# Modulation chunks in the router stage, and block-wise neighbourhood attention with its values reordered through DRAM

## What is computed

```python
def adaln(cond, w_mod, b_mod):
    m = jax.nn.silu(cond) @ w_mod + b_mod          # w_mod (1024, 6144) per layer
    return jnp.split(m[:, None, :], 6, axis=-1)

def neighbourhood_attention(q, k, v, k_ctx, v_ctx, rel_bias):   # 4 heads of 64
    # blocks of 16 query columns see 32 key columns kc0..kc0+31, all 8 rows
    kc0 = np.clip(j * 16 - 8, 0, 64 - 32)
    cs = np.clip(qcol - 8, 0, 64 - 16)
    col_mask = (kcol >= cs) & (kcol < cs + 16)
    s_loc = jnp.where(col_mask, q @ k_loc + bias, NEG_INF)
    s_ctx = q @ k_ctx                              # 128 cached context tokens
    pr = softmax(concatenate([s_loc, s_ctx]))
    return pr_loc @ v_loc + pr_ctx @ v_ctx
```

## Time and profile before

| | |
|---|---|
| three runs | 1847.62, 1848.31, 1857.03 us, median 1848.31 |
| the profiled execution | 1847.45 us, span 1845.6 us |
| TensorE busy | 1574.8 us (85%) |
| VectorE | 772.8 us (42%) |
| ScalarE | 471.4 us (26%) |
| GpSimd | 278.0 us (15%) |
| mean granted TensorE clock | 0.913 |
| DMA | 318.79 MB, 173 GB/s over the span |

### The profile page before, as it was taken

One profiled execution on the slowest core, in us unless ns is written; L12 is line 12 of the kernel. 1 busy time (PEld: TensorE's weight loads), 2 busy tenths in 40 slices (PEclk: granted clock), 3 DMA queues, 4 the chain that ended last, 5 costly groups with the idle time before them and its releaser, 6 DMA issues. The chain is left out here.

```text
span 1845.6 us, 23002 instructions
## 1 busy us (share of the span) xinstructions
PE 1574.8 (85%) x8725; PEld 987.4 (54%) x8725; DVE 772.8 (42%) x1586; ACT 471.4 (26%) x884; POOL 278.0 (15%) x446
## 2 busy tenths in 40 slices
PE   5899997975887976999689999996588796799993
PEld 3455554544886543444355555654488654444442
DVE  2379414454665241111254970364576524211116
ACT  1211122253322032222131111335432212222222
POOL 0200211015450012000102000001455101200002
PEclk9999999878899977999889999986798998799996
DMA  9521699913142009999581201351314200899974
GB/s 341 129 92 46 189 295 356 362 47 61 27 94 104 3 23 362 348 366 369 210 240 46 85 30 58 120 205 47 61 27 94 103 2 35 345 394 364 365 281 183
DMA packets 121264, 318.79 MB, mean 173 GB/s; under 512 B 29589, under 2 KB 39127, under 8 KB 106839
## 3 DMA queue, kind: packets, MB, share of 16 engines
q1 hardware_dynamic: 73264, 237.63, 37.4%
q0 software_dynamic: 14080, 53.48, 8.4%
q10 hardware_dynamic: 33830, 26.45, 5.2%
HBM read 250.70 MB, written 67.78 MB: 173 GB/s over the span
## 5 line engine op out<-in xcount | busy, mean ns | idle before, releaser
L741 PE MATMUL ps<-hreg,ring 128*128 128x512 f32 x768 | 396.9, 599 | 11.1 <-ACT hreg L1334 11.1
L742 PEld LDWEIGHTS ps<-hreg,ring 128*128 128x128 f32 x768 | 146.7, 191 | 185.5 <-issue 185.5
L1167 PE MATMUL ps<-ring,tok 128*128 128x512 f32 x544 | 236.4, 592 | 0.6 <-issue 0.5
L1167 PEld LDWEIGHTS ps<-ring,tok 128*128 128x128 f32 x544 | 103.2, 190 | 130.3 <-issue 130.3
L742 PE MATMUL ps<-hreg,ring 128*128 128x128 f32 x768 | 148.0, 275 | 0.0
L741 PEld LDWEIGHTS ps<-hreg,ring 128*128 128x128 f32 x768 | 117.5, 193 | 11.8 <-issue 11.8
L1182 PE MATMUL ps<-ring,work 128*128 128x512 f32 x272 | 123.4, 596 | 0.0
L2192 DVE TENSOR_TENSOR work<-work,ps 128x256 f32<-128x256 f32 x34 | 14.2, 421 | 250.5 <-ACT work L1618 250.5
L1755 DVE SCALAR_TENSOR_TENSOR mixA<-cin_reg,small,mixA 128x655 f32<-128x655 f32 x120 | 107.0, 894 | 0.0
L2196 DVE COPY zs<-ps 128x1024 f32<-128x1024 f32 x34 | 41.6, 1224 | 122.9 <-PE ps L1182 122.9
L2276 POOL TENSOR_TENSOR hreg<-dnT,cst 128x512 f32<-128x512 f32 x16 | 20.4, 1275 | 429.6 <-DVE dnT L1950 429.6
(11 more groups left out here) (353 smaller groups left out, 2630.9 us busy)
## 6 DMA issues: line engine op xcount, KB each, us to landing
ring<-in_w SPq DMA_DIRECT2D x102, 1024.0 KB, 8.7
ring<-in_w_mod SPq DMA_DIRECT2D x24, 2048.0 KB, 12.4
ring<-in_w_in SPq DMA_DIRECT2D x12, 2048.0 KB, 8.0
ys<-zs ACTq DMA_DIRECT2D x34, 512.0 KB, 7.8
tok<-xs SPq DMA_DIRECT2D x30, 512.0 KB, 11.8
xs<-zero POOLq DMA_DIRECT2D x8, 1792.0 KB, 19.7
ys<-zero POOLq DMA_DIRECT2D x8, 1664.0 KB, 20.3
ring<-diag_own SPq DMA_DIRECT2D x80, 128.0 KB, 5.2
```

Source lines behind the costliest of these rows:

```text
L741: mm(o[:, 0:TS], lhs(k), rhs(k)[:, 0:TS], start=k == 0, stop=k == nk - 1)
L742: ins = mm(o[:, TS:T], lhs(k), rhs(k)[:, TS:T], start=k == 0, stop=k == nk - 1)
L1167: ins = mm(bank(2 + q), xgT[q][:, k, :], w, start=k == 0, stop=k == KD - 1)
```

## The change

It moves and rewrites these parts:

1. **Start:** c is loaded ahead of x, and TensorE turns it first; ScalarE makes the Silu after 14 parameter DMAs, and issues three more and the bias copy (to 16 rows, not 64) behind it. VectorE makes five of layer 0's eight norm products before it copies modulation chunk 3, and clears the staging tiles after all eight, in both layers.
2. **Modulation chunks:** chunks 13, 14 and 15 leave attention for layer 0's router stage. Chunk 13 is loaded into `tok`, 14 into ring slot 1 and 15 into slot 2. ScalarE makes their copies. SP holds back expert weights until the slots are used.
3. **Attention:** a tile t is now 16 query columns by 8 rows. It sees 32 or 48 key columns (`KB0`, `KBN`: 2, 3, 3, 2 blocks of 16 columns by 8 rows), so 384 or 512 score columns with the cache. Q and K are put into block order by their eviction, the output back by its store.
4. **Values:** V leaves the projection in grid order; ScalarE stores it to DRAM (`v_rows`), waits, and loads it back as four blocks, on its own queue. TensorE's `values` waits for all of it.
5. **Bias tables:** eight loads with rows of 1,060 bytes, then 12 GpSimd additions.
6. **Zero fill:** GpSimd starts it after 6 gemms instead of 16.

The diff's core:

```diff
+ROUTER_MODS = (13, 14, 15)
 def mods_beside_attention(layer):
-    last = NMOD * (layer + 1) + (MOD_FIRST if layer + 1 < L else 0)
-    return list(range(NMOD * layer + MOD_FIRST, last))
+    return list(range(MOD_FIRST, ROUTER_MODS[0])) if layer == 0 else list(range(ROUTER_MODS[-1] + 1, 2 * NMOD))
...
# SP, router stage
                 up_load(0, 0)
                 need(mod2_ready, 2)
                 sp.dma_start(route_c, consts[:, NC:NC + NX]).then_inc(route_loaded.sem, 16)
+                if l == 0:
+                    need(gemm_done, G_OUT + 5)
+                    router_mod(13, tok_flat[:, 0:4096])
+                    router_mod(14, ring[1][:, 0:4096])
                 need(gemm_done, G_OUT + 8)
-                down_load(0, 0)
+                if l == 0:
+                    sp.wait_ge(mod_used, 14)
+                    router_mod(15, ring[2][:, 0:4096])
+                else:
+                    down_load(0, 0)
...
+                if l == 0:
+                    sp.wait_ge(mod_used, 15)
                 up_load(1, e)
+                if l == 0:
+                    sp.wait_ge(mod_used, 16)
+                    down_load(0, 0)
                 down_load(1, e)
...
# TensorE: first lines, attention, router
-            pe.wait_ge(once["first_loaded"], 64)
+            pe.wait_ge(once["cst_loaded"], 64)
+            turn(bank(4, 16), dsm[0:16, 0:P], ident[0:16, 0:16]).then_inc(once["cond_turned"], 1)
+            pe.wait_ge(once["first_loaded"], 32)
...
-                        mm(gslot(x)[:, 0:TS], qa[x], qkT[rs[x], 2 + h // 2, 0:TS], start=True, stop=True)
+                        mm(gslot(x)[:, 0:n], qa[x], qkT[rs[x], 2 + h // 2, P * KB0[t]:P * KB0[t] + n], start=True, stop=True)
...
-                    for j in range(NCH if i < 16 else 2):
+                    for j in range(KBN[i // 4] + 1 if i < 16 else 2):
                         ins = turn(ps[:, 2048 + P * j:2048 + P * (j + 1)], sc[i % 2][:, P * j:P * (j + 1)], ident)
...
                     if a < 8:
+                        need(kvc_loaded, 112)
                         need(att_ptc, 2 * a + 2)
...
                 ins.then_inc(logits.sem, 1)
+                if l == 0:
+                    mod_rows(13, 7)
+                    mod_turn(13, later_rows[1], 3200)
                 need(sel_ready, 1)
...
                 need(slots_ready, 1)
+                if l == 0:
+                    mod_rows(14, 2)
+                    mod_rows(15, 3)
+                    need(slots_ready, 2)
+                    mod_turn(14, later_rows[0], 3208)
+                    mod_turn(15, later_rows[1], 3216)
                 need(xf_loaded[0], 16)
...
# ScalarE: second norm, V, before the experts
+                        if n == 1 and l == 0 and k == 2:
+                            act.wait_ge(mod_used, 14)
+                            A_(later_rows[1], bank(7), ACT.Copy).then_inc(mod_copied, 1)
...
-                A_(vna.rearrange("p t n -> p (t n)"), ps[:, 2048:2048 + NCH * NAW], ACT.Copy).then_inc(v_copied.sem, 1)
+                A_(v_own, ps[:, 2048:2048 + 4 * NAW], ACT.Copy)
+                A_(vna[:, 4, :], ps[:, 2048 + 4 * NAW:2048 + NCH * NAW], ACT.Copy).then_inc(v_copied.sem, 1)
+                need(v_copied, 1)
+                need(kvc_loaded, 32)
+                act.dma_start(v_rows.ap()[l].rearrange("(t p) n -> p t n", p=P), v_own.rearrange("p (t n) -> p t n", t=4))\
+                    .then_inc(kvc_loaded.sem, 16)
                 need(newk_turned, 1)
                 A_(newk, ps[:, 3584:3584 + 256], ACT.Copy).then_inc(newk_copied.sem, 1)
+                need(kvc_loaded, 48)
+                for b in range(4):
+                    src = bass.AP(tensor=v_rows, offset=(l * TS + 16 * b) * NAW, ap=[[GRID * NAW, 8], [NAW, 16], [1, NAW]])
+                    act.dma_start(vna[:, b, :], src).then_inc(kvc_loaded.sem, 16)
...
+                if l == 0:
+                    for n, bnk in ((14, 2), (15, 3)):
+                        act.wait_ge(mod_used, n + 1)
+                        if n == 15:
+                            act.wait_ge(mod_turned, 14)
+                        A_(later_rows[n % 2], bank(bnk), ACT.Copy).then_inc(mod_copied, 1)
                 copy_tokens(0, 0)
                 copy_tokens(0, 1, 2048)
...
# ScalarE, eviction of Q and K
-                    evac(G_QK + t, qkT[:, t, :]).then_inc(gemm_out[t % 2].sem, 1)
+                    if t == 0:
+                        need(tz_ready, 1)
+                    out = qkT[:, t, 0:TS].rearrange("p (b r c) -> p r b c", r=8, c=16)
+                    for r_ in range(0, 8, 4):
+                        A_(out[:, r_:r_ + 4], by_block(gslot(t % 2)[:, 0:TS])[:, r_:r_ + 4], ACT.Copy)
+                    A_(qkT[:, t, TS:T], gslot(t % 2)[:, TS:T], ACT.Copy).then_inc(gemm_out[t % 2].sem, 1)
...
# VectorE: start, attention
+                early = 5 if l == 0 else 0
                 if l == 0:
                     for n in range(MOD_FIRST):
+                        if n == MOD_FIRST - 1:
+                            need(norm_r, 1)
+                            for k in range(early):
+                                norm_one(k)
                         mod_copy(n, 4 + n % 2, first_rows[n])
...
+                need(norm_r, 1)
+                for k in range(early, KD):
+                    norm_one(k)
                 for s in stage:
                     V.memset(s, 0.0)
                 V.memset(cin_reg[:, :], 0.0).then_inc(pads_zeroed.sem, 1)
...
-                        V.scalar_tensor_tensor(s[:, 0:TS], o[:, 0:TS], HD ** -0.5, Tz[:, b * GRID:b * GRID + TS], ALU.mult, ALU.add)
+                        V.scalar_tensor_tensor(s[:, 0:n], o[:, 0:n], HD ** -0.5, biases[t][:, h, :], ALU.mult, ALU.add)
...
+                if l == 0:
+                    dve.wait_ge(mod_turned, ROUTER_MODS[-1] + 1)
+                    V.tensor_copy(mod_next[:, 8:32], ps[:, 3200:3224])
# GpSimd
-                    pool.wait_ge(gemm_done.sem, gemm_done.at(0, G_Z))
+                    pool.wait_ge(gemm_done.sem, gemm_done.at(0, G_DN + 2))
```

More of the change, by code:

```diff
@@ L66, in ring_table @@
             held[s] = item
+        if layer == 0:
+            for n, s in zip(ROUTER_MODS, (2, 1, 2)):
+                count[s] += 16
+                slot[("mod", n)], value[("mod", n)] = s, count[s]
         up_base.append(list(count))
@@ L333, in build, with bias_window, by_block, att_cols @@
         tok_flat = tok[:, :, :, :].rearrange("p a c n -> p (a c n)")
[L334 to L336 removed]
+        WB = 7 * CO + 48
+        wide_bias = work[:, 0:NH * WB]
+        def bias_window(h, first, nb):
+            at0 = wide_bias[:, WB * h + first:WB * h + first + 16]
+            return bass.AP(at0.tensor, at0.offset, [at0.ap[0], [16, nb], [CO, 8], [1, 16]])
+        biases, at_ = {}, 0
+        for j in (1, 0, 3):
+            n = 8 * 16 * KBN[j]
+            biases[j] = tok_flat[:, at_:at_ + NH * n].rearrange("p (h n) -> p h n", h=NH)
+            at_ += NH * n
+        biases[2] = biases[1]
+        sc = [tok_flat[:, at_ + 512 * i:at_ + 512 * (i + 1)] for i in range(2)]
+        v_own = hreg[:, 0:4 * NAW]
+        def by_block(ap):
+            return ap.rearrange("p (r b c) -> p r b c", r=8, c=16)
+        def att_cols(i):
+            return P * KBN[i // 4]
         dflat = dnT[:, :, :].rearrange("p a b -> p (a b)")
@@ L689, in mod_rows @@
                 def mod_rows(n, bnk):
-                    w = loaded(("mod", n))[:, 0:4096].rearrange("p (k n) -> p k n", k=KD)
+                    held = loaded(("mod", n))
+                    if n == ROUTER_MODS[0]:
+                        held = tok_flat
+                    w = held[:, 0:4096].rearrange("p (k n) -> p k n", k=KD)
                     for k in range(KD):
@@ L846, in values @@
                     if a < 8:
+                        need(kvc_loaded, 112)
                         need(att_ptc, 2 * a + 2)
-                        for j in range(NCH):
+                        nb, first = KBN[a // 2], KB0[a // 2]
+                        for j in range(nb + 1):
                             for x in range(2):
                                 h = 2 * (a % 2) + x
-                                va = vna[:, j, 64 * h:64 * h + 64] if j < 4 else kvc[1][:, 64 * h:64 * h + 64]
-                                ins = mm(halves[x], va, pT_[x][:, P * j:P * (j + 1)], start=j == 0, stop=j == NCH - 1)
+                                va = vna[:, first + j, 64 * h:64 * h + 64] if j < nb else kvc[1][:, 64 * h:64 * h + 64]
+                                ins = mm(halves[x], va, pT_[x][:, P * j:P * (j + 1)], start=j == 0, stop=j == nb)
                     else:
```

139 lines of the change are left out of this document (73 added, 66 removed).

## The result

The changed kernel takes 1839.57 us (median of six runs, 1832.03 to 1843.96), the kernel before 1852.32 beside it (six runs, 1847.62 to 1857.24): a ratio of 0.9921, 95% interval 0.9892 to 0.9949. Its profiled execution took 1837.82 us (span 1836.0, mean clock 0.912), 9.63 less than that of before; forecast were 24.5. By the medians the gain is 12.8 us.

What follows compares the result with a forecast made beforehand. Expert loops and projections keep TensorE busy; the edits target four places where it waits or shares, layer 0's attention on DMA filled by zero fill. 1847.45 - 4.2 - 2.2 - 5 - 14.7 + 1.5 = 1822.9, said 1823; range 1810 to 1840.

Steps and rivals of the forecast that it cites:

- step 6: Layer 1's narrower attention: 4.4 us saved beside chunks swallowed by chunk supply, 8.7 saved after them; layer -5 us in all.
- step 7: Layer 0's attention, nine chunks instead of twelve: 80.6 us from V's end against 95.3, -14.7 us (bounds -8 and -21).
- step 5: V's trip through DRAM after the V projection: first value matmuls +6.7 us later in each layer (bounds +1 and +15).
- Step 3: Zero fill started after 6 gemms, 88 us earlier, beside input chunks loaded two ahead: costed at 0.
- Rival (b): Chunk supply bounds more, or zero fill still runs into it; half of layer 0's gain stays out: 1830, chance 0.14.
- breaking point: Sign that the forecast is wrong: a hole behind V's store of over 12 us.
- Rival (a): V's trip through DRAM is longer, 8 us a layer more than forecast: 1839, chance 0.16.
- rival (d): TensorE does not warm up in attention and its work beside chunks runs at the lower clock: 1870, chance 0.08.
- The slow part: Layer 1's attention after its last chunk: narrower score widths save 8.7 us.
- Step 8: Layer 0's router stage with chunks 13 to 15: later weight loads and scatters, +1.5 us (bounds -1 and +8).
- rival (c): Router stage: expert weights behind chunks 14 and 15 arrive late: 1830, chance 0.08.
- Steps 1, 2 and 4: Kernel start -4.2 us; layer 1's start with memsets moved behind -2.2; bias tables and reordering evictions nothing.

Runs made afterwards that it cites:

- half the bytes: Changed kernel with half of each modulation chunk's weights loaded, all matmuls kept: 1865.5 us, ratio 1.0076; put right for two extra pairs of expert blocks, 1819.8.
- the repeat: The changed kernel itself, unedited, measured once more beside the others: 1834.5 us, ratio 0.9903.
- chunk rows in the hole: Changed kernel with each modulation chunk one turn earlier, the first chunk's rows meant to run during V's trip through DRAM: 1862.2 us, ratio 1.0058.
- no trip: Changed kernel with V copied straight into the value matmuls' operand, no store or loads: 1793.8 us; put right for one fewer pair of expert blocks, 1816.7.
- ScalarE's copies first: Changed kernel with ScalarE doing two copies of turned probabilities and the third head's Exp before waiting for V's store: 1840.3 us, ratio 0.9948.

## Why the prediction was right and wrong

**The failed term** is the sum of steps 6 and 7: -19.7 predicted for the two attentions, -9.0 measured. Of the 10.7 us that are missing, 4.9 are layer 1's chunk part (step 6), 3.9 the hole behind V in both layers (step 5), 0.7 the slow part and 1.2 the rest of layer 0. Outside attention the router stage misses 2.2 us, the two starts 1.2, and 0.8 lie in stages that nobody forecast a move for.

**Step 3, the zero fill at nothing.** The mechanism was read rightly, a late chunk in layer 0 and no attention beside the fill once it is moved, and the cover held: input chunks loaded two ahead took it without a wait. But the gain was put down to the narrower attention in step 7, and the edit alone was never summed. Alone it is worth 12.5 us in layer 0's attention, more than the whole change gained there. Rival (b) took the zero fill for something that might go wrong; it was the part that went right.

**Step 5, V through DRAM, at +6.7.** Measured from the kernel before it is +8.4 and +8.9; against the changed kernel without the trip it is 9.7 and 11.7, 21 us in all, since narrower attention without the trip would have started its values sooner than before (7.9 and 6.3 for 9.2 and 9.0). Two sub-terms were short in layer 1: the store 8.2 us for 6.5, the issues 4.0 for 2.8 (the two cache stores were left out of them). The rule that store and chunk share one pool was right; the rate was not: 387 GB/s were taken, and the windows of the hole show 337 and 353. By the fit of the Trainium skill (DMA: Bandwidth & Descriptors, "Anatomy of one DMA") the hole would have been smaller than forecast; that fit holds only for the store that has no chunk beside it (above). TensorE's idle time in the hole, 11.7 and 12.3 us, stands at the bound that the prediction named as its breaking point. Rival (a), a longer trip, gives the time that was measured (1839), but by 8 us more a layer where 2 were found: right in kind, and in size by coincidence.

**Step 6, the chunk part.** Predicted 34.4 us from the first values on, measured 39.3 and 36.1; with half the bytes 34.3. What failed is "the 4.4 us are swallowed": a supply that is a little too slow can do more than swallow. It makes one wait of about 2 us, and in the changed kernel's profile 3 more go at the lower clock behind it; in the repeat they do not. So a part of the miss is chance, and what decides whether the clock falls behind such a wait no run here shows. This is rival (d) in small, where all or nothing had been asked.

**The slow part**: -8.7 predicted, -8.0 measured. **Layer 0** the same sum: 80.6 predicted, 83.5 measured. The hole is 1.7 of the 2.9; a late chunk at 331.0 (2.0 us of wait, rows at 2.46 us) can account for the other 1.2, which nothing separates.

**Step 8, the router stage**: +1.5 predicted, +3.7 measured, 3.8 given back when the chunks go back. The cover was there and the chunks lie in it. What was late is what was not named: the gathered rows themselves, whose second block now comes 3.0 us behind the first. Expert weights (rival (c)) are not what TensorE waits for at 702. Over all profiles the stage takes 121.8 to 124.7 us with the chunks in it and 118.5 to 121.3 without. Which of the moved loads delays the rows was not tried.

**Steps 1, 2 and 4**: -3.8 for -4.2 and -1.4 for -2.2, and nothing for the tables. The start repeats badly: in twelve profiles of the new order the first projection matmul comes between 49.3 and 55.9 us, 51.7 on average, against 53.9 and 54.4 in the two of the old, so that its own gain may be 2 to 3 rather than 4. The stretch between the layers is 42.0 to 43.3 us in eleven of the twelve (47.6 with the chunk rows in the hole), against 44.0 and 44.7.

So the column blocks did not earn their price as built: the narrowing gives 7 to 9 us a layer (no trip against before, with the zero fill moved: 73.9 for 82.8, with three chunks less, and 71.7 for 78.4 to 80.9), and the trip takes 10 to 12. With the trip held clear of the third chunk it takes 4 to 5, and the kernel is the fastest of those tried, though by less than the intervals tell from the kernel before with the zero fill and the starts.

## What to carry to other kernels

When a change has several edits, price each alone against the kernel before, above all the small one that clears the DMA engines: here one line alone is worth as much as the whole, and the large part does not pay for the transfer that it needs. A round trip through DRAM on the critical path is priced by what else is on the DMA engines at that moment, whichever queue issues it; with the bulk load held back for those few microseconds, the store took 3 us where it had taken 8 to 9. And where TensorE's work gets narrower, give the sum a range for what its short waits do to the clock: here the same wait was followed by the lower clock in one execution and not in the next.

## What the runs showed of the hardware

The 512 KB store of V took 3.0 us with no chunk beside it, 8.0 to 9.3 beside a 2 MB load, 9.8 with a second chunk asked for in the hole, and 14.0 beside one such load and the zero fill. Four loads of 128 KB took 2.6 to 3.0 us to issue and 5.4 beside the zero fill. It is not the full DMA engines alone that slow the issuing: with ScalarE's copies first the same four took 2.99 us beside a chunk, with the DMA share at 1.03 over them (from 1184.95), and beside the zero fill 5.44 at 1.00.

Waits of 2.0 us for VectorE in every pair stood beside a granted clock of 0.50 to 0.84 over 50 us in layer 0, and beside 1.00 from 1233 to 1253 in layer 1 of the same execution (chunk rows in the hole). A wait of 2.0 us for one chunk was followed by the lower clock (1215.02, rows at 2.46 us), and one of 1.85 in the repeat was not (1215.28, 1.92). After an idle stretch of 12 us the first chunk's rows took 3.08 us (1186.58), and the work behind them ran at full speed.
